# x plus the gated sum of the first 31 expert pairs formed by GpSimd during the last pair; VectorE adds the last pair's gated tiles to x straight from PSUM

## The reference, cut to what matters

```python
h = _rmsnorm(x, norm2_g) * (1.0 + sc2) + sh2
x = x + g2 * _moe(h, ...)          # 64 experts, 8 for each token, plus a shared expert
y = _rmsnorm(x, final_norm_g)      # the output
```

## Time and profile before

| what | value |
|---|---|
| median of 3 runs | 983.5 us (983.16 to 984.31) |
| span of the profiled execution | 981.3 us |
| PE busy | 933.0 us, 95% |
| DVE busy | 500.8 us, 51% |
| ACT busy | 211.7 us, 22% |
| POOL busy | 52.0 us, 5% |

### The profile page before, as it was taken

One profiled execution on the slowest core, in us unless ns is written; L12 is line 12 of the kernel. 1 busy time (PEld: TensorE's weight loads), 2 busy tenths in 40 slices (PEclk: granted clock), 3 DMA queues, 4 the chain that ended last, 5 costly groups with the idle time before them and its releaser, 6 DMA issues.

```text
span 981.3 us, 11669 instructions
## 1 busy us (share of the span) xinstructions
PE 933.0 (95%) x4219; PEld 433.9 (44%) x4251; DVE 500.8 (51%) x1045; ACT 211.7 (22%) x405; POOL 52.0 (5%) x68
## 2 busy tenths in 40 slices
PE   4999999999999999988999999999999999999991
PEld 2446444855655545833433334343434343433330
DVE  3202520785677664641545454545545454545457
ACT  4111201210000013501222222222222222222212
POOL 1010000100000000001000000000000000000000
PEclk9999999999999999978999999999999999999997
DMA  9993222304546711189999999999999999999911
GB/s 331 391 333 130 86 85 86 118 1 173 213 173 256 255 46 43 70 336 420 422 422 421 422 419 420 421 419 419 413 422 419 419 419 420 416 417 415 420 74 65
DMA packets 63994, 285.82 MB, mean 291 GB/s; under 512 B 6344, under 2 KB 6528, under 8 KB 38720
## 3 DMA queue, kind: packets, MB, share of 16 engines
q1 hardware_dynamic: 57216, 265.56, 67.2%
q0 software_dynamic: 6720, 19.50, 5.2%
HBM read 286.24 MB, written 3.80 MB: 296 GB/s over the span
## 4 chain that ended last, share of the span: by engine, by line
PE 91%; DMA 4%; DVE 2%; ACT 1%; issue 1%; SPq 0%; DVEq 0%; POOLq 0%; ACTq 0%
PE bank L1063 22%; PE bank L674 15%; PE bank L1096 12%; PE bank L1089 12%; PE bank L667 11%; PE bank L856 4%; PE bank L999 2%; DMA ring<-in_w_in 2%; PE bank L897 2%; PE bank L690 2%; PE bank L1002 2%; PE bank L1074 1%; DMA VG<-h_rows,idx 1%; DMA QK<-h_rows,idx 1%; PE bank L942 1%; PE bank L722 1%
## 5 line engine op out<-in xcount | busy, mean ns | idle before, releaser
L1063 PE MATMUL bank<-ring,QK 128*64 128x512 f32 (+1 forms) x1184 | 225.3, 592 | 0.0
L1063 PEld LDWEIGHTS bank<-ring,QK 128*64 128x64 f32 (+1 forms) x1184 | 72.5, 130 | 147.5 <-issue 147.5
L1096 PE MATMUL bank<-Fm,VG 128*128 128x512 bf16 x544 | 122.8, 379 | 6.5 <-DVE Fm L1967 3.0
L1952 DVE TENSOR_TENSOR hT<-bank,hT 128x512 f32<-128x512 f32 x192 | 118.1, 682 | 3.7 <-PE bank L1096 2.6
L1089 PE MATMUL bank<-ring,VG 128*64 128x512 f32 (+1 forms) x592 | 118.3, 603 | 0.5 <-ACT VG L1410 0.5
L667 PE MATMUL bank<-ring,hT 128*128 128x512 f32 x240 | 103.8, 593 | 0.0
L1943 DVE SCALAR_TENSOR_TENSOR VG<-VG,cw,bank 128x256 f32<-128x256 f32 x32 | 15.4, 481 | 144.5 <-issue 138.1
L1961 DVE TENSOR_TENSOR Fm<-bank,Fm 128x512 f32<-128x512 f32 x64 | 44.3, 692 | 85.0 <-ACT Fm L1417 85.0
L1096 PEld LDWEIGHTS bank<-Fm,VG 128*128 128x128 bf16 x576 | 56.0, 98 | 66.6 <-DVE Fm L1967 3.7
L674 PE MATMUL bank<-hT,ring 128*128 128x384 f32 x256 | 85.4, 487 | 0.0
L1417 ACT CAST Fm<-bank 128x512 bf16<-128x512 f32 x64 | 37.5, 586 | 208.7 <-PE bank L1089 208.7
(11 more groups left out here) (367 smaller groups left out, 821.1 us busy)
## 6 DMA issues: line engine op xcount, KB each, us to landing
ring<-in_w_exp_gate SPq DMA_DIRECT2D x64, 1024.0 KB, 13.7
ring<-in_w_exp_up SPq DMA_DIRECT2D x64, 1024.0 KB, 16.7
ring<-in_w_exp_down SPq DMA_DIRECT2D x64, 1024.0 KB, 15.0
ring<-in_w_ada SPq DMA_DIRECT2D x12, 2048.0 KB, 10.5
ring<-in_w_in SPq DMA_DIRECT2D x10, 2048.0 KB, 17.0
ring<-in_w_four_out SPq DMA_DIRECT2D x2, 2048.0 KB, 7.8
ring<-in_w_out SPq DMA_DIRECT2D x2, 2048.0 KB, 11.1
ring<-in_w_ret_out SPq DMA_DIRECT2D x1, 2048.0 KB, 13.7
```

The source lines that it names most:

```text
L1063: ins = mm(ps[0][rows, :], xT[:, k, rows], expert(2 * s + n)[0][:, k, :, :], start=(k == 0), stop=(k == KC - 1))
L1096: ins = mm(ps[banks[g]][:, :], slotT[:, k, t * P:(t + 1) * P], y[:, h * 512:(h + 1) * 512], start=(n == 0), stop=(n == 2))
L1952: v.tensor_tensor(into, o, into, ALU.add).then_inc(sem("summed"), 1)
```

## The change

Three things change.

1. POOL gets twelve instructions behind its last gather. For each of the six tiles, as soon as DVE has added pair 30's tile to `y_sum` (`summed`), POOL multiplies it by the gate into `work[:, 0:512]` (semaphore `sum_gated`) and adds that to x in place (`x_summed`). All are 128x512 float32 with both inputs in SBUF.
2. DVE no longer adds pair 31's tiles to `y_sum`. In `sums_to_x`, for each tile it multiplies the PSUM bank by the gate into one of two 128x512 buffers (`gated`), raises `summed`, waits for POOL's `x_summed` of this tile, and adds the buffer to x.
3. The read of the number of extra rounds and the branch on it stand ahead of pair 31's sums instead of behind them. Where there are no extra rounds (the `Else` side) the odd tiles' additions raise `x2_ready` themselves, and `residual` is gone. The three final norms follow together behind all six tiles. Where there are rounds, they sum into the cleared `hTf`, which is gated and added at the end as before.

```diff
+        gated = [work[:, 512:1024], DTf[:, 1024:1536]]
...
+            for t in range(TT):
+
+                for n in range(2):
+                    cut = slice(n * 512, (n + 1) * 512)
+                    pool.wait_ge(sem("summed"), 6 * (PAIRS - 1) + 2 * t + n + 1)
+                    if t or n:
+                        pool.wait_ge(sem("x_summed"), 2 * t + n)
+                    nc.gpsimd.tensor_tensor(work[:, 0:512], y_sum[:, t, n, :], g2_rows[:, min(t, 1), cut], ALU.mult).then_inc(sem("sum_gated"), 1)
+                    pool.wait_ge(sem("sum_gated"), 2 * t + n + 1)
+                    nc.gpsimd.tensor_tensor(x[:, t, cut], x[:, t, cut], work[:, 0:512], ALU.add).then_inc(sem("x_summed"), 1)
...
+            def sums_to_x(p, even, odd):
+
+                for g in range(6):
+                    t, cut = g // 2, slice(g % 2 * 512, (g % 2 + 1) * 512)
+                    added = sem(odd if g % 2 else even)
+                    dve.wait_ge(sem("scattered"), p * 6 + (g + 1))
+                    if g > 1:
+                        dve.wait_ge(added, g // 2)
+                    v.tensor_tensor(gated[g % 2], ps[IN_ORDER[g]][:, :], gate[t][:, cut], ALU.mult).then_inc(sem("summed"), 1)
+                    dve.wait_ge(sem("summed"), p * 6 + (g + 1))
+                    dve.wait_ge(sem("x_summed"), g + 1)
+                    v.tensor_tensor(x[:, t, cut], x[:, t, cut], gated[g % 2], ALU.add).then_inc(added, 1)
...
-            sums(LAST - 1)
...
-            further_rounds(dve, further)
-
-            def residual(t):
-                cut = slice(t * D, (t + 1) * D)
-                link(v.tensor_tensor(work[:, :], hTf[:, cut], gate[t], ALU.mult))
-                v.tensor_tensor(x[:, t, :], x[:, t, :], work[:, :], ALU.add).then_inc(sem("x2_ready"), 1)
-                dve.wait_ge(sem("x2_ready"), t + 1)
...
+            dve.wait_ge(sem("table_ready"), 1)
+            n_rounds = dve.value_load(tab_rounds, min_val=0, max_val=FURTHER)
+            with dve.If(n_rounds > 0):
+                sums_to_x(LAST - 1, "x_even", "x_odd")
+                dve.wait_ge(sem("x_even"), TT)
+                dve.wait_ge(sem("x_odd"), TT)
+                rounds_to_x()
+            with dve.Else():
+                sums_to_x(LAST - 1, "x_even", "x2_ready")
...
-            residual(0)
-            for t in range(1, TT):
-                residual(t)
-                final_norm(t - 1)
-            final_norm(TT - 1)
+            for t in range(TT):
+                final_norm(t)
```

More of the change, by code:

```diff
@@ L2036, in further, with rounds_to_x @@
                 sums(p)
-            further_rounds(dve, further)
-            def residual(t):
-                cut = slice(t * D, (t + 1) * D)
-                link(v.tensor_tensor(work[:, :], hTf[:, cut], gate[t], ALU.mult))
-                v.tensor_tensor(x[:, t, :], x[:, t, :], work[:, :], ALU.add).then_inc(sem("x2_ready"), 1)
-                dve.wait_ge(sem("x2_ready"), t + 1)
+            def rounds_to_x():
+                for t in range(TT):
+                    v.memset(hTf[:, t * D:(t + 1) * D], 0.0).then_inc(sem("sums_cleared"), 1)
+                dve.wait_ge(sem("sums_cleared"), TT)
+                with dve.Fori(0, n_rounds) as q:
+                    further(q)
+                stand_alone(dve, "rounds_done")
+                for t in range(TT):
+                    v.tensor_tensor(work[:, :], hTf[:, t * D:(t + 1) * D], gate[t], ALU.mult).then_inc(sem("round_gated"), 1)
+                    dve.wait_ge(sem("round_gated"), t + 1)
+                    v.tensor_tensor(x[:, t, :], x[:, t, :], work[:, :], ALU.add).then_inc(sem("x2_ready"), 1)
+                    dve.wait_ge(sem("x2_ready"), t + 1)
+            dve.wait_ge(sem("table_ready"), 1)
[7 more added lines that the diff above has]
+                sums_to_x(LAST - 1, "x_even", "x2_ready")
             def final_norm(t):
```

## The result

The changed kernel takes 995.6 us (median of 5 runs, 992.95 to 997.51) against 983.5 for the kernel before: a ratio of 1.0121 (95% interval 1.0101 to 1.0140), some 12 us slower. The prediction was 984.1 us with a range up to 986.2. It was wrong: the loss is over three times the largest cost that its sum held (3.72 us).

A forecast was written before the change was run, and what follows sets the result against it. It took the tail, DVE's chain behind PE's last scatter, as the bound: 3.09 us saved on DVE against 3.72 us of exclusion with POOL, DVE ending 0.63 us later, so 983.5 became 984.1 us, range 980.0 to 986.2.

The forecast's parts named there:

- the largest cost that its sum held: Delay of DVE in the tail under exclusion: 1.57 for the low parts and 2.15 for the additions, 3.72 us.
- POOL starts when pair 30's first tile is summed: Start of POOL's twelve instructions: 950.44 + 0.69, with the semaphore about 951.20 us.
- twelve POOL instructions of about 1.2 us from 951 on: Sign expected in the timeline after the change, showing POOL's gating and adding of pair 30's tiles.
- Rival (c): DVE's wait for `x_summed`: POOL's chain becomes the bound, kernel slower; at 2.0 us an instruction 987.9 us; chance 0.15.
- POOL 1.2 us an instruction with 0.10 between: POOL's 128x512 steps in the tail: 0.69 x 1.73 = 1.19 us each, 0.10 us between dependent instructions.
- the ratio of 1.73: POOL's time over DVE's for fills of 128x1, 102 ns against 59, used to scale 0.69 us to 1.19.
- Exclusion: POOL and DVE's two-SBUF-input instructions: whichever reads second waits for the other's whole instruction; 984.1 us, chance 0.50.
- Its walk: Step-by-step tail under exclusion: low parts 1.57 us late, additions 2.15, DVE ends at 978.91 us.
- The DVE tail without POOL: DVE from the first scattered tile to the last norm, POOL's part free: ends at 975.19, 3.1 us sooner, 980.4 us.
- 12 x 0.73: DVE's six gatings and six additions of pair 31, each waiting for the one ahead: 8.76 us.
- The branch costs nothing: Round counter and branch ahead of the sums: 0.57 us, covered by DVE's 0.92 us before PE's first tile.
- ACT stays hidden: Three norms in a row: ACT's square is read 1.43 us behind the variance, DVE busy until 1.90; hidden by 0.47 us.

The follow-up runs named there:

- e3: Kernel before plus sixteen unused POOL multiplications of 128x512 reading two SBUF tensors, from pair 30's first sum on: 988.66 us, ratio 1.0059.
- e8: Kernel before plus 32 unused POOL fills of 128x512 that read nothing, from pair 30's first sum on: 982.65 us, ratio 1.000.
- e1: Changed kernel with POOL's wait count put right, 6 * (PAIRS - 2) instead of 6 * (PAIRS - 1): 980.71 us, ratio 0.9985 to the kernel before.
- e4: Changed kernel without POOL's twelve instructions; DVE gates and adds pair 30's sums itself in six of 128x1024: 983.68 us, ratio 1.0003 to the kernel before.
- e5: e1 with POOL's sixth instruction held until both low parts of pair 31 are written: 980.33 us, ratio 0.9981 to the kernel before; again 980.19.
- e2: Changed kernel with POOL's wait the constant 187 at every tile, late but without turns: 989.63 us, ratio 1.0072 to the kernel before.
- e9: e1 with four unread float32 matmuls of 128x512 on PE ahead of the last scatter: 982.01 us, ratio 0.9993 to the kernel before.

## Why the prediction was wrong, point by point

- **POOL starts when pair 30's first tile is summed, about 951.20.** This step failed, and with it the forecast. I took it from the words of the change and from the shape of the wait and never counted what `summed` stands at; 6 x 31 + 1 = 187 against 186 at the end of pair 30 was to be read in the code. POOL started 0.78 us behind DVE's first gating of pair 31, 10.4 us later than the count that was meant would have let it. Of the signs that I had named, this one failed: "twelve POOL instructions of about 1.2 us from 951 on". A rival "it doesn't do what it says" was missing. With it the sum is short: six tiles of 4.09 us and three norms, 24.5 + 5.5 = 30.0 us from the first gating, against 17.46 before, 12.5 us more.
- **Rival (c), POOL's chain becomes the bound at `x_summed`.** The place was right, the reason wrong. It asked for a POOL instruction of 1.8 us or more (about 1.4 with exclusion); one took 1.26 us, and POOL bound the kernel because it began 10.4 us late and then waited for DVE at each tile.
- **POOL 1.2 us an instruction with 0.10 between.** Right: 1.26 and 0.08. But the way there was lucky: the ratio of 1.73 came from fills of one element on each partition, and nothing showed that it holds for 512 elements and two inputs (1.26 / 0.69 is 1.83). The Trainium skill's figure (GPSIMD Engine Reference, section 3.1), from which I had estimated 1.12 us, was a little low for this form.
- **Exclusion.** Right as a mechanism (e3, e8). Its walk gave 1.57 us for the low parts; e1 shows 1.67 (3.13 - 1.46). For the additions it gave 2.15; e1 shows 0.80 + 3 x 1.05 - 4 x 0.69, 1.2 us. The walk let an instruction start only when the other had ended, and so end 0.69 us behind it. In e1's records DVE's second addition ends 0.56 us behind POOL's instruction (964.31 + 1.05 against 963.20 + 1.60), so a collision costs 0.35 us and not 0.43, and the first addition met POOL's instruction near its end. Missing was PE's clock, 0.64 us ahead of the first tile in e1.
- **The DVE tail without POOL, 3.09 us shorter.** Right in kind, too small: 3.96 us in e4. The mis-sized term is 12 x 0.73. A gating doesn't wait for the addition ahead of it and starts 0.61 us after its start (965.45 to 966.06), so a tile costs 1.33 us, six of them 7.97 us instead of 8.76. The norms took 5.53 us instead of 5.61.
- **The branch costs nothing.** Right: DVE idles 0.92 us ahead of its first gating after as before, released by PE.
- **ACT stays hidden.** Right: the norms follow at 1.8 us each (982.74, 984.55 and 986.37 in the trace of after).

Put together, what the change was described to do is worth -3.96 + 1.67 + 1.2 + 0.64 = -0.45 us; e1's tail shows 29.56 - 30.05 = -0.49. My forecast for it had +0.6, so it stood near the described kernel. Luck had a part in that: the delays sum to 3.5 us against my 3.72 because what I had too much for the additions (0.95 us) was in good part made up by PE's clock (0.64 us), which I hadn't foreseen. And it was a forecast of e1 and not of the changed kernel.

## What to carry to other kernels

Where engines are held together by counting semaphores, work out the absolute count at each new wait and name the instruction that reaches it, before costing anything: one pair off here put 15 us of work that should have been hidden onto the path and made two engines take turns. A wait inside a loop that asks for one count more in each step, and whose partner waits for the loop's output, is a turn-taking loop; its cost is the sum of both engines, whatever either's busy share says. Work moved to GpSimd is hidden only if its SBUF reads don't meet VectorE instructions with two SBUF inputs on the path; a pause around those was worth 0.46 us here (e5), and it helps only as far as GpSimd's remaining work isn't then the bound.

## What the runs showed of the hardware

- A POOL instruction that reads SBUF and a DVE instruction with two SBUF inputs exclude each other, either way round (e2 for POOL as the second, e5 for DVE). The loser's record starts and stretches: DVE's 128x512 from 0.69 to as much as 1.75 us, DVE's 128x1024 from 1.22 to 2.17, POOL's 128x512 from 1.26 to 1.79 (2.13 for one in e3). No idle time appears, so the views of waits don't show it; the longest duration of a group against its median does (e3):

```profile
L1974 DVE TENSOR_TENSOR Fm<-Fm x64: 680/691/1746, 457.1 to 957.2; 128x512 bf16<-128x512 f32 x64
```

- POOL fills of 128x512 (0.525 us each) beside the same DVE instructions cost nothing.
- PE's granted clock was 0.50 at the start of the scatter behind 4.75 us of standing still (e3), 4.88 (e1) and 8.10 (e4, with POOL idle), and 1.00 with fillers up to 1.10 us ahead (e9). In e5 it was 1.00 at the start and fell to 0.50 about 1 us into the scatter, behind 2.81 us of standing still; e8 kept 1.00 behind the same 2.81. (The 3.03 of before is the same stretch: its trace has only 17 of the scatter's 18 matmuls, and the first one is the one that is missing.) In e5 the fall cost nothing, because DVE took longer than PE for each tile; in e3 it did, since DVE waited 0.59 and 0.39 us for the second and third tile. What decides it beyond the standing still is left open.
